# One program per engine for setup, both layers and the end of an encoder step

## The reference, cut to what matters

```python
for i in range(DEPTH):          # DEPTH = 2, each for hp (prompt) and hs (sample)
    h = x + 0.5 * rmsnorm(swiglu(rmsnorm(x, f1_pre), f1_up, f1_down), f1_post)
    mix, new = token_mix(rmsnorm(h, m_pre), ...)   # conv, HGRN, window and stick-breaking attention
    h = h + rmsnorm(mix, m_post)
    h = h + 0.5 * rmsnorm(swiglu(rmsnorm(h, f2_pre), f2_up, f2_down), f2_post)
    e = pe.astype(h.dtype) @ ple_w
    h = h + rmsnorm(e * jax.nn.sigmoid(rmsnorm(h, ple_pre) @ ple_gate_w), ple_post)
```

## Time and profile before

| | |
|---|---|
| median of 3 runs (lowest to highest) | 3511.64 us (3510.53 to 3516.72) |
| the profiled execution, its own time | 3519.2 us |
| its span, first to last instruction | 3517.5 us |
| PE busy | 3266.0 us, 93% of the span |
| DVE, ACT, POOL busy | 1386.8, 1096.2, 1206.1 us |
| granted TensorE clock, mean | 0.957 |

### The profile page before, as it was taken

How to read it: one execution, slowest core, us unless ns; L and a number is a source line. 1 busy time by engine, 2 the same in 40 slices (tenths; PEclk the granted TensorE clock), 3 DMA queues, 4 the chain that set the end, 5 groups by cost and what they waited for, 6 DMA issues and landing times. The chain is left out here.

```text
span 3517.5 us, 56480 instructions
## 1 busy us (share of the span) xinstructions
PE 3266.0 (93%) x23523; PEld 3105.9 (88%) x23523; DVE 1386.8 (39%) x1793; ACT 1096.2 (31%) x1518; POOL 1206.1 (34%) x538
## 2 busy tenths in 40 slices
PE   8999998877999999999889999988789999999997
PEld 7999986776699899999789999867676998999987
DVE  4222144784444323312333321548844433332133
ACT  3332231124533333323233322311255333333232
POOL 4333442131134433344333334411211434333442
PEclk9999998998999999999899999989899999999988
DMA  3222211121122122232022222111210221222211
GB/s 95 83 81 82 83 57 49 37 77 51 31 66 78 55 83 78 82 89 75 13 85 82 79 84 83 54 41 44 67 53 26 78 82 56 82 79 87 83 59 40
DMA packets 455963, 236.25 MB, mean 67 GB/s; under 512 B 18630, under 2 KB 454150, under 8 KB 455814
## 3 DMA queue, kind: packets, MB, share of 16 engines
q1 hardware_dynamic: 445792, 227.05, 22.1%
q10 hardware_dynamic: 10022, 7.15, 0.7%
HBM read 228.53 MB, written 5.63 MB: 67 GB/s over the span
## 5 line engine op out<-in xcount | busy, mean ns | idle before, releaser
L1832 POOL TENSOR_TENSOR wlo<-wraw,whi 128x1024 fp32r<-128x1024 f32 x432 | 1076.3, 2492 | 2122.3 <-ACT whi L503 2122.3
L536 PE MATMUL ps<-u_hi,whi 128*128 128x288 f32 x4800 | 1062.2, 302 | 36.3 <-ACT ybr L1565 11.8
L536 PE MATMUL ps<-u_lo,whi 128*128 128x288 f32 x4800 | 1038.2, 297 | 0.0
L536 PE MATMUL ps<-u_hi,wlo 128*128 128x288 f32 x4800 | 1037.2, 297 | 0.0
L536 PEld LDWEIGHTS ps<-u_hi,whi 128*128 128x128 f32 x4800 | 778.4, 191 | 73.3 <-issue 33.0
L536 PEld LDWEIGHTS ps<-u_lo,whi 128*128 128x128 f32 x4800 | 779.5, 190 | 0.0
L536 PEld LDWEIGHTS ps<-u_hi,wlo 128*128 128x128 f32 x4800 | 778.0, 190 | 0.0
L503 ACT ACTIVATE whi<-wraw 128x1024 fp32r<-128x1024 f32 x432 | 456.9, 1058 | 959.0 <-PE ps L536 958.5
L783 DVE TENSOR_TENSOR sq<-sq,ps 128x576 f32<-128x576 f32 x88 | 66.4, 754 | 751.0 <-PE ps L536 751.0
L536 PE MATMUL ps<-s_hi,wlo 128*128 128x288 f32 x1408 | 302.7, 296 | 0.0
L536 PE MATMUL ps<-s_lo,whi 128*128 128x288 f32 x1408 | 302.7, 296 | 0.0
(11 more groups left out here) (277 smaller groups left out, 2985.3 us busy)
## 6 DMA issues: line engine op xcount, KB each, us to landing
wraw<-in_ffn_up SPq DMA_DIRECT2D x176, 512.0 KB, 3.8
wraw<-in_w_in SPq DMA_DIRECT2D x104, 512.0 KB, 3.8
wraw<-in_ffn_down SPq DMA_DIRECT2D x64, 512.0 KB, 3.8
wraw<-in_ffn_down SPq DMA_DIRECT2D x32, 384.0 KB, 3.3
wraw<-in_w_out SPq DMA_DIRECT2D x16, 512.0 KB, 3.8
wraw<-in_ple_gate_w SPq DMA_DIRECT2D x16, 512.0 KB, 3.8
wraw<-in_w_branch SPq DMA_DIRECT2D x16, 256.0 KB, 2.7
xtok<-in_x_prompt SPq DMA_DIRECT2D x4, 512.0 KB, 6.6
```

What stands on the lines that cost most here:

```text
L536: ins = pe.matmul(ps[:, 2 * p + f, 0:HT], wt[:, part, w], x[:, k, HT * f:HT * f + HT], start=start and n == 0 and c == 0, stop=stop and n ...
L1832: pool.tensor_tensor(wlo[:, i % SPLIT, :], wraw[:, i % RAW, :], whi[:, i % SPLIT, :], ALU.subtract).then_inc(w_split, 1)
```

## The change

Setup, the two layers and the end become functions that each engine calls one after the other in a single block. The loop over layers is gone: the layer's code stands twice, with the layer's number fixed in it. No semaphore is cleared; every wait in a layer has `before(s)` added, which is 0 in layer 0 and in layer 1 the number by which that semaphore rose in layer 0 (table `IN_LAYER`). Parameters are read in place, so the seven copies per layer are gone.

Some work moves. ACT rounds the first two weight units of layer 1, and POOL splits them, inside the last 8 units of layer 0. SP's loads follow the loads of `x` directly, so the first weight units come during setup; a scratch of the setup leaves `wraw` for a place of its own. The forget bound's arithmetic stands behind the first norm of layer 0. ACT's squares of `h` at a layer's start wait for each tile by itself. In the end PE turns the first three blocks of tokens tile by tile as the residual delivers them, the copies are shared by DVE (3) and ACT (2), and the result has a buffer `otok` of its own.

The core of the diff, with its indentation evened and the added `before(...)` shown at a few places:

```diff
 def done(i):
-    return i + 1 + SPLIT
+    return UNITS * L + i + 1 + SPLIT
+def before(s):
+    return L * IN_LAYER[s]
 def load_unit(sp_, slot, i, src, n=8):
-    sp_.wait_ge(w_split, i + 1)
+    sp_.wait_ge(w_split, i + 1 + UNITS * L)
 def act_square_h(act, n, k):
-    if n:
+    if n or L:
         if k in ADD_POOL:
-            act.wait_ge(h_ready_pool, len(ADD_POOL) * (n // 2 - 1) + ADD_POOL.index(k) + 1)
+            act.wait_ge(h_ready_pool, len(ADD_POOL) * (n // 2 - 1) + ADD_POOL.index(k) + 1 + before(h_ready_pool))
         ...
+    else:
+        act.wait_ge(placed, k + 1)
 def act_ffn(act, L, f, u0):
     ...
     if f == 0:
+        if L == 0:
             act_round(act, 0)
             act_round(act, 1)
     act_norm_root(act, 4 * f + N_F1PRE)
+    if f == 0 and L == 0:
+        bounds_scalar(act)
 def act_ple(act):
     ...
-    if m + 2 < KD:
+    if m + 2 < KD or L < DEPTH - 1:
         act_round(act, U0_PLEG + m + 2)
 # POOL
-    straight(U0_PLEG + 2, UNITS)
+    straight(U0_PLEG + 2, UNITS + (2 if L < DEPTH - 1 else 0))
     pool_residual(pool, N_PPOST)
-with nc.Fori(0, DEPTH) as L:
-    with nc.Block() as block:
-        ...
-        dve.tensor_copy(gains[:].rearrange("p (n l k) -> p n l k", n=8, l=1), gains_all[:, :, ly, :]).then_inc(par_ready, 1)
-        ...                              # seven such copies
-    with nc.Block() as block:
-        ...
-                for x in per_layer:
-                    dve.sem_clear(x)
+def end_tensor(pe):
+    def turn(t, k):
+        n = min(128, T - 128 * t)
+        at = t if t < 4 else 0
+        return pe.transpose(ps[0:n, 2 * at + k // 4, 128 * (k % 4):128 * (k % 4) + 128], h[:, k, 128 * t:128 * t + n], ident[:])
+    pe.wait_ge(std_ready, 8 * DEPTH)
+    for k in range(KD):
+        ...                              # wait for tile k of h, from POOL or DVE
+        for t in range(3):
+            ins = turn(t, k)
+            if k == KD - 1:
+                ins.then_inc(tok_turned, 1)
+    for t in (3, 4):
+        if t == 4:
+            pe.wait_ge(tok_placed, 1)
+        for k in range(KD):
+            ins = turn(t, k)
+        ins.then_inc(tok_turned, 1)
+def end_vector(dve):
+    for t in (0, 2, 4):
+        dve.wait_ge(tok_turned, t + 1)
+        dve.tensor_copy(*end_place(t)).then_inc(tok_placed, 1)
+def end_scalar(act):
+    for t in (1, 3):
+        act.wait_ge(tok_turned, t + 1)
+        act.activation(*end_place(t), ACT.Copy).then_inc(tok_kept, 1)
+with nc.Block() as block:
+    @block.tensor
+    def _(pe):
+        pe.sem_inc(unit_done, SPLIT)
+        setup_tensor(pe)
+        pe.wait_ge(consts_done, n_consts[0])
+        pe.wait_ge(placed, n_placed[0])
+        for _, _, layer_tensor, _, _ in layers:
+            layer_tensor(pe)
+        end_tensor(pe)
+    ...                                  # the other four engines likewise
```

More of the change, by code:

```diff
@@ L486, in done @@
-        def done(i):
-            return i + 1 + SPLIT
-        def dmas(i):
-            return 4 if U0_PAIR <= i < U0_OUT and (i - U0_PAIR) % 3 == 0 else 2 if i - U0_PROJ in (SQ_, SQ_ + 1) else 1
-        def landed(i):
-            return 16 * sum(dmas(j) for j in range(i % RAW, i + 1, RAW))
-        def act_round(act, i, it=0):
-            act.wait_ge(w_loaded[i % RAW], it * 16 + landed(i))
-            act.wait_ge(unit_done, it * 4 + done(i - SPLIT))
-            act.activation(whi[:, i % SPLIT, :], wraw[:, i % RAW, :], ACT.Copy).then_inc(w_rounded, 1)
@@ L527, in products @@
-        def products(pe, part, x_hi, x_lo, ks, k_off, p, start, stop, wait_k=None):
-            ins = None
-            for n, k in enumerate(ks):
-                if wait_k is not None:
-                    wait_k(k)
-                w = slice(128 * (k_off + n), 128 * (k_off + n) + 128)
-                for c, (wt, x) in enumerate(((whi, x_hi), (whi, x_lo), (wlo, x_hi))):
-                    for f in range(2):
-                        ins = pe.matmul(ps[:, 2 * p + f, 0:HT], wt[:, part, w], x[:, k, HT * f:HT * f + HT],
-                                        start=start and n == 0 and c == 0, stop=stop and n == len(ks) - 1 and c == 2,
-                                        skip_group_check=True)
-            return ins
@@ L738, in dve_apply @@
-        def dve_apply(dve, n):
-            dve_rstd(dve, n)
-            for k in range(KD):
-                dve.scalar_tensor_tensor(out=uf[:, k, :], in0=h[:, k, :], scalar=gains[:, 8 * n + k:8 * n + k + 1],
-                                         in1=flat(3), op0=ALU.mult, op1=ALU.mult).then_inc(u_full, 1)
-                if k and k - 1 in LO_DVE:
-                    low(dve, n, k - 1, u_ready)
-            low(dve, n, KD - 1, u_ready)
-        def add_to_h(engine, n, k, signal):
-            engine.wait_ge(y_normed, 8 * (n // 2) + k + 1)
-            engine.tensor_tensor(h[:, k, :], h[:, k, :], uf[:, k, :], ALU.add).then_inc(signal, 1)
@@ L1944 @@
+                setup_sync(sp_)
+                for layer_sync, _, _, _, _ in layers:
+                    layer_sync(sp_)
+                end_sync(sp_)
 OUTS = [
```

2676 lines of the change are left out of this document (1366 added, 1310 removed).

## The result

| us | before | changed |
|---|---|---|
| median of the runs of this comparison | 3511.09 | 3455.68 |
| range of the runs | 3502.98 to 3516.72 | 3455.31 to 3457.03 |
| profiled execution: time, span | 3519.2, 3517.5 | 3455.7, 3454.0 |

The ratio is 0.9845, 95% interval 0.9825 to 0.9864: 55.4 us faster by the medians, where 28.5 were forecast.

What follows compares the result with a forecast made beforehand. PE, busy 93% of the span, bounds the kernel, so time can be won only where it waits or at the ends: 4.7 + 10.6 + 13.2 = 28.5 us off the median 3511.64 gives 3483.1 us, range 3477 to 3491.

Steps and rivals of the forecast that it cites:

- all three places: Setup to layer 0, layer 0 to layer 1, and layer 1 to the end: holes of 4.2, 13.36 and 9.8 us.
- the new waits: End of layer 0: last add 0.7 us more behind POOL's split, PE sum 1.75 us later and at the low clock.
- Term A: Setup to layer 0: first sum of squares and PE sum start earlier, 4.7 us, between 4.0 and 5.6.
- the fast sum (0.84 us): Setup to layer 0: PE sums at the high clock, 1.28 us instead of 2.12, taken as term A's upper end.
- the diagonal's collision: First norm of layer 0: DVE's diagonal still collides with POOL's split and takes 2.46 us as now.
- Term B: Layer 0 to layer 1: layer 1's PE sum 12.0 us earlier, less 0.84 and 0.5, so 10.6 us; ends 9.0 and 13.5.
- the slow sum: PE sum at layer 0's end: low clock after PE has stood still for longer, 0.84 us.
- Term C: Layer 1 to the end: turns and copies start earlier, last store issues sooner; 13.2 us, between 12.3 and 13.7.
- the half-kept hole: Between the layers: half the 13.36 us is instruction fetching and stays, B loses 6.7 us, 3489.8 us; chance 0.10.
- the starved PE: Whole span: the longer straight program makes PE wait for instruction packets, 0.5 us each, 3534 us; chance 0.04.
- does not do what it says: Any of the places: another wait takes the meeting's place, 3488 to 3496 us, or 3511 for no change; chance 0.06.
- The sums stay fast: Layer 0's start and between layers: no low clock, no wait behind POOL; upper ends, 3478.8 us; chance 0.10.

Runs made afterwards that it cites:

- b_64: Kernel before with 64 unused bytes between the rounded weights and all that follows; 3489.09 us against 3516.63, ratio 0.9925.
- a_wpad: Changed kernel with 576 unused bytes ahead of the rounded weights, so weights and moving operands move together; one run, 3454.8 us.
- b_keep: Kernel before with three more clock-keeping products behind each of the first seven sums of the last pre-norm (PPRE); 3515.25 us, ratio 0.9996.
- b_ushift: Kernel before with the four small parameter buffers placed behind `u_lo`, so `u` lies as in the changed kernel, `s` as before; 3499.35 us, ratio 0.9940.
- a_pad: Changed kernel with 576 unused bytes ahead, so `u`, `s` and the norm buffers lie as in the kernel before; 3479.46 us, ratio 0.9894.
- a_keep: Changed kernel with three more clock-keeping products behind sums of all pre-norms but the first, and 24 more between the layers; 3482.31 us, ratio 0.9896.
- a_bound: Changed kernel with 24 more clock-keeping products between the layers and eight more before each PPOST norm's sum; 3455.04 us, ratio 0.9827.
- a_conv: a_bound with 60 more clock-keeping products ahead of the convolution's sums; 3455.69 us, ratio 0.983.
- a_meetclear: a_meet with a further block between the layers in which DVE clears an unused semaphore 98 times; one run, 3476.7 us.
- a_meet: a_noround cut into four blocks with meetings of all engines between setup, layers and end, no clearing, no loop; 3465.44 us, ratio 0.9875.
- a_noround: Changed kernel with the moved roundings and splits back at layer 1's start; one run, 3458.0 us.

## Why the prediction was off, point by point

- **What was forecast happened, and nearly at its size.** Time went from all three places and the new waits came where I had put them. The edit proper gave 30.8 us (b_64's span less the changed kernel's), against 28.5. That the sum is so near is in part luck: two terms were too small and one too large.
- **The step that failed** is the sentence "The bodies of the layers are PE's own and have the same instructions after the change. So the sum is made of three terms." The instructions are the same, their operands' places are not. The diff showed it: four buffers go, in front of `u_hi`. 20,352 products at about 1 ns are 20 us, more than any of my terms, and the price is set by the distance to the weights (a_wpad, b_64). In the medians b_64 gives 27.5 us, which holds the norm's gain too.
- **The norm's clock** was the second miss, 5.1 and 5.3 us in the profiled runs and the 1.1 us behind its root. b_keep shows that the clock made it slow. Why the clock falls there in both traces of the kernel before and not in those of b_ushift, a_pad or b_64 is not shown; in these PE reaches the norm 5 to 13 us earlier in the span, and the norm itself is the same.
- **Term A was mis-sized**: 4.7 forecast; 5.05 to the PE sum, but 8.2 to the first `uf`. I took the fast sum (0.84 us) as an upper end, yet left the clock-keeping records at 4.82 and the diagonal's collision as it was. The low clock was more than the sum: before, it was granted from 32 to 42 us, over the sum, the diagonal's spread and most of the clock-keeping records, and was back at 1.00 before the first products; after, it is 1.00 from 27 us on. Before:

```profile
32.00:42.00 10.00, 8.42 (x33) 7.09 (x33) 5.23 (x6) 1.82 (x4) 4.49 (x3) 0.50 0.37 107
44.00:46.00 2.00, 2.00 (x17) 2.00 (x16) 2.00 (x3) 0.61 (x1) 1.97 (x2) 1.00 0.00 0
```

  The diagonal lost 0.47 us and not 1.64, since it started at 28.55 beside the first of the two splits, near its end, and not at the start of the second. It was done at 29.84, 0.69 us behind the first split's end (26.80 + 2.35), as it was done 0.68 us behind the second one's end before.

- **Term B held**: PPOST root to layer 1's root fell by 13.9 us, where my own steps (7.0 us from last tile to PE sum, then a slow sum) give 13.7; the measured 6.6 and 2.29. The stretch ahead of it grew by 1.0 and not by 2.6. From the last gate to the root it did grow by 2.5: the rounding, 0.54 us behind POOL's split, and the slow sum. But the gate products start 1.1 us earlier behind the norm that is no longer slow, and gain 0.4 by their pace. The reason I gave for the slow sum is wrong, and that it came is luck. I had put the low clock down to a longer pause of PE; in layer 1, where nothing was moved, the pause is the same as before and the sum is slow all the same (b_64 has 2.29 us behind 2.64 too). Before and changed:

```profile
3481.10 1.28 PE L559 MATMUL ps<-ones,sqsum 128*128 128x1 f32 x10 [2.64 <-DVE sqsum L720]
```

```profile
3428.28 2.29 PE L601 MATMUL ps<-ones,sqsum 128*128 128x1 f32 x10 [2.63 <-DVE sqsum L765]
```

  The Trainium skill's lock of SBUF between DVE and GpSimd (SBUF — State Buffer, "Who interferes with whom") agrees here: 1.30 us for an add of 0.76 that starts inside a split. The clearing was the largest part of the hole, 8.5 of 13.4 us, and the jump 3.2; I had not told them apart, and I had counted the parameter copies as part of the gain, where ACT's table load and square covered them.
- **Term C was 1.5 us too high**: 21.8 less 10.1 is 11.7, below my lower end of 12.3. The copies end 4.3 us behind the tile (forecast 4.6); from the issue of the last store to the end it is then 5.2 us, where I had carried over the 3.4 of a store that has the queues to itself.
- **The rivals**: the half-kept hole, the starved PE and "does not do what it says" are out: DVE doesn't stand between the layers any more, and instruction packets are 100 with 1.64 MB, as good as before. "The sums stay fast" was right for layer 0 and wrong between the layers.

The sum over the profiled runs, by what was measured: A 8.2, B 12.9, C 11.7, pace 20, norm clock 10.4 make 63 us, against spans that differ by 63.5.

## What to carry to other kernels

When a change adds or drops a buffer, write down where every operand behind it will lie, above all relative to the weights: the longest loops pay for it, and no order of instructions shows it. To read a pace of 1 ns in 130, take the spacing of the rows that drain the products and divide by the count; the mean duration hides it. Before prices are put on a hole, split it into meeting, clearing and jump with a row each: an idle time called issue can be full of the sequencer's own rows, and reading the lines of the clears and of the branch would have split this one before any run. And more clock-keeping gained nothing in any of its four trials here (b_keep, a_keep, a_bound, a_conv): look first whether PE is idle where it would stand, and whether PE, not another engine, sets the end there.

## What the runs showed of the hardware that I had not expected

- Products of 128x288 (float32 rounded form, a weight load beside each) start each 133.2 to 133.3 ns where the moving operand lies 0, 32 or 96 above a multiple of 128 bytes from the weights, and each 132.2 ns at 64. It holds for `u` (0 and 64) and for `s` (all four) apart, and moving the operands and the weights together by 576 bytes changes nothing. The Trainium skill (TensorE: Matmul & The Clock Gate, "Back-to-back issue gap") gives N / 2.4 + 2.5 ns for a product by itself, by which 288 columns would take an estimated 122.5 ns, and says that in a stream with weight loads both operations set the spacing; both measured values are longer, and the page has no term for addresses. What collides in the slow case no run here shows.
- In the window from 1716 to 1722 us of the changed kernel PE is busy 5.95 of 6.00 us, with clock-keeping among its records, and its granted clock is 0.50; in a_conv 60 such products, which ended 2 us before the sums behind them, did not bring these to the high clock:

```profile
1716.00:1722.00 6.00, 5.95 (x21) 4.67 (x21) 1.01 (x2) 1.55 (x2) 0.00 (x0) 0.50 0.31 90
```

- Clearing 98 semaphores one by one on DVE, with a meeting, takes 8.8 us (a_meetclear). A meeting of all engines by itself takes 0.5 to 0.7 us until the next instruction (a_meet), and cost 1.5 to 4.5 us by place through the work that could not run ahead of it. The jump back over a layer's code stood for 2.6 us on ACT and 3.2 on DVE (the kernel before).
- A DVE instruction with two SBUF inputs of 0.82 us alone took 1.29 to 2.85 us when it started beside a POOL split, and was done 0.68 to 0.69 us behind the end of that split each time (the kernel before, changed, a_noround, a_meetclear).
